# A hybrid streaming layer on one core: in the stream of attention units a tile's outputs are turned three steps behind their unit in place of two, and turns of stored and cached keys move by a step

## The chip, the core and the metric

The kernel runs on one core of a Trainium2 chip. The metric is the device time of the whole program in microseconds; lower is better. Engines are named as in the profile: PE is TensorE (matmuls, and transposes, which are matmuls with an identity), PEld its weight loads, DVE is VectorE, ACT is ScalarE, POOL is GpSimd, SP is SyncE, which only issues transfers here.

## What is computed

One inference step of one transformer layer on 1024 prompt rows and 64 new rows, with d = 1024, all in float32:

```
h = rmsnorm(x, g_mix)
qa, ka, va, qb, kb, vb, forget, gate_a, gate_b = split(h @ w_in + b_in)
A = sliding-window attention with sinks and relative bias   (8 query heads, 2 key heads, 64 wide)
B = forgetting attention, logit[t,s] += c[t] - c[s], c = cumsum(log_sigmoid(forget)), causal (8 heads)
x = x + (sigmoid(gate_a) * (A @ w_oa) + sigmoid(gate_b) * (B @ w_ob)) @ w_out
x = x + SwiGLU(rmsnorm(x));   y = rmsnorm(x, g_final)
outputs: y, and the new rows of keys, values and log forgets (kb and vb token by token)
```

The new rows also attend to 2048 cached rows of keys and values.

## The kernel before

Every large product is split: each operand is a sum of a high and a low part, and a product is three matmuls (lines L2247, L2248, L2249). The input product has 34 blocks of 128 columns in three pieces each; a piece is 24 matmuls of 320 or 384 columns. This change lies in the part of the program that the code calls the stream of units, from about 118 to 612 us of the trace.

A unit is one head of one tile of 128 queries. There are 136 units in the stream: units 0 to 71 are sliding-window ("swa"), in pairs of heads over nine tiles; units 72 to 135 are forgetting attention ("fox"), in pairs of heads over eight tiles, the later tiles with more keys. Units 2k and 2k + 1 are the two heads of one tile, and their outputs lie side by side in one slot of `o_tok`. Four units more follow the stream, for the new rows against the cache.

PE works through steps n = 0 to 135. In a step it does, in this order:

1. `turn(n)`: transposes the probabilities of unit n (L2328);
2. `scores(n + 2)`: query times keys (L2310, and L2314 for the causal mask);
3. the turns listed for this step in the table `turns_at` (below);
4. in even steps one piece of the input product ("dense", L2247 to L2249), some 3.5 to 4 us long;
5. `outputs(n - 1)`: probabilities times values (L2351) into bank 6 of `ps`.

So an odd step is short, and an even step holds a long block of matmuls that wait for nothing. The other engines follow the same steps. DVE in step n: copies half of the groups of transposed probabilities out (L562), adds the bias to scores n + 2 and takes the maximum (L1546, L1552), evacuates this step's turns (`turned_lo`), splits keys, queries or weights on some steps (L1493, L1529), and then scales the output of unit n - 1 into `o_tok` (`normalise`, L1577). ACT in step n: exp of unit n + 1 (L1086), evacuates the piece of the step before (L1073), copies the other half of the groups (L562), and makes the high parts of this step's turns (`turned_hi`).

The table has three kinds of turns, and all go through one bank, bank 7:

- `ot`, for odd n: the 128x128 slot of `o_tok` of units n - 1 and n is transposed (PE, L2363), ACT writes `ot_hi` (L1098), DVE writes `ot_lo` (L1601). POOL saves rows of them to DRAM (L893).
- `tok`, for a block of keys or values in three parts: four transposes for parts 0 and 1 (L2370), one for part 2 (L2372), then a DVE copy into `tokst` (L1589 or L1591), which POOL stores (L884, L886). ACT has no part in it.
- `cache`: four transposes of cached keys (L2377), two ACT casts (L1103), then two DVE subtractions (L1526).

Two waits of PE matter. Before any turn PE waits until the turn before it in the list has left bank 7 (`misc_done`). Before an `ot`, and before `outputs(n)`, it waits until `normalise` has written the outputs of the units ahead (`o_evac`): `ot` of unit n wants those of unit n, and `outputs(n)` wants those of unit n - 1, since all share bank 6:

```python
if k:
    pe.wait_ge(misc_done, k)
...
    pe.wait_ge(o_evac, ev[1] + 1)
...
if n >= 1:
    pe.wait_ge(o_evac, n)
```

Of the kernel before, what the change touches and what calls it, by code (L numbers as in the profile page):

```python
# [49 lines left out]
B_QA, B_KB, B_VB, B_QB, B_GATE = 2, 6, 10, 14, 18  # L50
# [57 lines left out]
N_STREAM = 136  # L108
# [81 lines left out]
def build_program(nc, x_prompt, x_sample, cache_swa_k, cache_swa_v, cache_fox_k, cache_fox_v, cache_fox_logf,  # L190
# [38 lines left out]
    with ExitStack() as ctx:  # L229
# [271 lines left out]
        turns_at = {step: [] for step in range(N_STREAM)}  # L501
        for n in range(1, N_STREAM, 2):
            if n + 2 < N_STREAM:
                turns_at[n + 2].append(("ot", n))
        for i in range(8):
            for part in range(3):
                turns_at[6 * i + 4 + 2 * part].append(("tok", B_KB + i, part))
        for c in range(4):
            turns_at[126 + 2 * c].append(("cache", 0, c))
        order = [ev for step in range(N_STREAM) for ev in turns_at[step]]  # L510
        order.append(("ot", N_STREAM - 1))
        for s in range(4):
# [2259 lines left out]
```

## Time and profile before

| | |
|---|---|
| device time, median of 3 runs | 1637.95 us (1637.29 to 1638.94) |
| the profiled execution | 1638.05 us, of which the span is 1636.3 us |
| PE busy | 1602.3 us, 98% of the span |
| DVE busy | 1018.6 us, 62% |
| ACT busy | 666.5 us, 41% |
| granted clock of PE | 0.998 of full speed over the span |

The device time is longer than the span by the 1.75 us that lie around it. Busy time of PE counts a matmul until its modelled end, and a next one starts before that; so a PE busy for 98% can still start matmuls later than it could. Starts, not busy time, are to be compared.

### The profile page before, as it was taken

The numbers are of one execution on the slowest core, as the hardware profiler recorded it, in microseconds if no ns is written. First come the engines' busy times: TensorE is split into PE (matmuls) and PEld (weight loads), VectorE is DVE, ScalarE is ACT, GpSimd is POOL, SyncE is SP. The second block draws the span as 40 slices with busy tenths as digits, with TensorE's granted clock in tenths as the row PEclk, the third lists the DMA queues.
The fourth block names the chain that finished last, engine by engine and source line by source line (L and its number), as shares of the span: only waits on it lengthen the run. The fifth ranks groups of instructions, "written<-read, shape, count | busy, mean of one in ns | idle before, by whom it ended". The sixth has DMA issues, their size and how long they took to land.

```text
span 1636.3 us, 27700 instructions
## 1 busy us (share of the span) xinstructions
PE 1602.3 (98%) x10556; PEld 1504.0 (92%) x10556; DVE 1018.6 (62%) x2232; ACT 666.5 (41%) x1333; POOL 174.7 (11%) x312
## 2 busy tenths in 40 slices
PE   7999999999999999999999999999999999999997
PEld 6999999999999999988898799999999999888886
DVE  6646555655546554436366686776677777579865
ACT  5334444544445444334253552222232222434453
POOL 3011111000000001012011000000122222110000
PEclk9999999999999999999999999999999999999999
DMA  7052331553341424659455333322344444776432
GB/s 209 26 163 100 123 109 67 185 171 92 118 138 59 123 92 149 197 185 326 151 175 177 122 91 94 118 87 73 102 156 157 157 157 150 265 229 189 144 124 89
DMA packets 190290, 230.59 MB, mean 141 GB/s; under 512 B 14807, under 2 KB 140280, under 8 KB 189640
## 3 DMA queue, kind: packets, MB, share of 16 engines
q1 hardware_dynamic: 163616, 138.71, 28.8%
q0 software_dynamic: 26544, 90.12, 15.5%
q8 instruction: 85, 1.39, 0.3%
q14 instruction: 45, 0.37, 0.1%
HBM read 166.76 MB, written 62.08 MB: 140 GB/s over the span
## 4 chain that ended last, share of the span: by engine, by line
PE 91%; DVE 4%; DMA 2%; issue 1%; ACT 1%; POOL 0%; SPq 0%; DVEq 0%; ACTq 0%; POOLq 0%
PE ps L2247 24%; PE ps L2248 24%; PE ps L2249 24%; PE ps L2351 7%; PE ps L2310 4%; PE ps L2328 3%; PE ps L2363 1%; PE ps L2532 1%; PE ps L2531 1%; DMA w_raw<-in_w_gu_dram 1%; PE ps L2269 1%; DMA w_raw<-in_w_ob_dram 1%; DVE e_lo L1897 1%; PE ps L2370 1%; PE ps L2389 0%
## 5 line engine op out<-in xcount | busy, mean ns | idle before, releaser
L2247 PE MATMUL ps<-h_hi,w_hi 128*128 128x384 f32 (+1 forms) x816 | 274.6, 337 | 1.4 <-DVE h_lo L1518 1.4
L2249 PE MATMUL ps<-h_hi,w_lo 128*128 128x384 f32 (+1 forms) x816 | 267.1, 327 | 0.0
L2248 PE MATMUL ps<-h_lo,w_hi 128*128 128x384 f32 (+1 forms) x816 | 266.9, 327 | 0.0
L2247 PE MATMUL ps<-t_hi,e_hi 128*128 128x272 f32 x704 | 202.6, 288 | 1.1 <-DVE silu L1912 1.1
L2248 PE MATMUL ps<-t_lo,e_hi 128*128 128x272 f32 x704 | 202.8, 288 | 0.0
L2249 PE MATMUL ps<-t_hi,e_lo 128*128 128x272 f32 x704 | 202.1, 287 | 0.0
L2247 PEld LDWEIGHTS ps<-h_hi,w_hi 128*128 128x128 f32 x816 | 154.1, 189 | 3.4 <-DVE h_lo L1518 1.7
L2247 PE MATMUL ps<-b_hi,e_hi 128*128 128x272 f32 x528 | 152.6, 289 | 4.5 <-ACT p L1367 1.7
L1577 DVE TENSOR_SCALAR o_tok<-ps,rinv 128x64 f32<-128x64 f32 x136 | 38.6, 284 | 189.1 <-PE ps L2351 186.9
L2248 PEld LDWEIGHTS ps<-h_lo,w_hi 128*128 128x128 f32 x816 | 154.1, 189 | 0.5 <-issue 0.5
L2249 PEld LDWEIGHTS ps<-h_hi,w_lo 128*128 128x128 f32 x816 | 153.7, 188 | 0.0
L2248 PE MATMUL ps<-b_lo,e_hi 128*128 128x272 f32 x528 | 152.1, 288 | 0.0
L2249 PE MATMUL ps<-b_hi,e_lo 128*128 128x272 f32 x528 | 151.7, 287 | 0.0
L2247 PEld LDWEIGHTS ps<-t_hi,e_hi 128*128 128x128 f32 x704 | 132.7, 188 | 1.3 <-DVE e_lo L1897 1.3
L2249 PEld LDWEIGHTS ps<-t_hi,e_lo 128*128 128x128 f32 x704 | 132.5, 188 | 0.0
L2248 PEld LDWEIGHTS ps<-t_lo,e_hi 128*128 128x128 f32 x704 | 132.4, 188 | 0.0
L1073 ACT ACTIVATE stg<-ps,bin_cols 128x384 f32<-128x384 f32 (+1 forms) x96 | 54.0, 562 | 186.9 <-PE ps L2249 186.8
L1086 ACT ACTIVATE sprob<-sprob,negm 128x256 f32<-128x256 f32 (+8 forms) x140 | 92.3, 659 | 73.5 <-DVE negm L1552 73.0
L2249 PE MATMUL ps<-e_hi,f_lo 128*128 128x512 f32 x308 | 119.8, 389 | 0.0
L2248 PE MATMUL ps<-e_lo,f_hi 128*128 128x512 f32 x308 | 119.8, 389 | 0.0
L2247 PE MATMUL ps<-e_hi,f_hi 128*128 128x512 f32 x308 | 119.8, 389 | 0.0
L1493 DVE TENSOR_TENSOR w_lo<-w_raw,w_hi 128x1024 fp32r<-128x1024 f32 x66 | 80.6, 1221 | 53.8 <-ACT w_hi L1041 53.7
(338 smaller groups left out, 3605.1 us busy)
## 6 DMA issues: line engine op xcount, KB each, us to landing
w_raw<-in_w_gu_dram SPq DMA_DIRECT2D x104, 256.0 KB, 3.3
w_raw<-in_w_in_dram SPq DMA_DIRECT2D x68, 256.0 KB, 3.2
zg_d<-stg POOLq DMA_DIRECT2D x28, 544.0 KB, 3.0
act_d<-act POOLq DMA_DIRECT2D x44, 272.0 KB, 2.8
s_d<-s_sum POOLq DMA_DIRECT2D x44, 256.0 KB, 3.4
f_raw<-s_d SPq DMA_DIRECT2D x44, 256.0 KB, 2.8
f_raw<-act_d SPq DMA_DIRECT2D x33, 256.0 KB, 2.9
w_raw<-in_w_out_dram SPq DMA_DIRECT2D x32, 256.0 KB, 3.6
```

The costliest lines, as they stand in the source:

```text
L1073: nc.scalar.activation(out, ps[:, bank_of(p), 0:c1 - c0], ACT.Identity, bias=bin_cols[:, col:col + 1]) \
L1086: nc.scalar.activation(probs, probs, ACT.Exp, bias=negm[0:R, c], accum_out=rowsum[0:R, c]).then_inc(p_ready, 1)
L1493: nc.vector.tensor_tensor(w_lo[:, slot, :], w_raw[:, slot, :], w_hi[:, slot, :].bitcast(F32), ALU.subtract) \
L1577: ins = nc.vector.tensor_scalar(o_tok[0:R, tl, HD * e:HD * e + HD], ps[0:R, 6, 0:HD], rinv[0:R, c], None, ALU.mult)
L1897: nc.vector.tensor_tensor(e_lo[:, q % RING, :], src, e_hi[:, q % RING, :].bitcast(F32), ALU.subtract) \
L2247: nc.tensor.matmul(out, l_hi, r_hi, start=start, stop=False)
L2248: nc.tensor.matmul(out, l_hi, r_lo, start=False, stop=False)
L2249: return nc.tensor.matmul(out, l_lo, r_hi, start=False, stop=stop)
L2269: last = nc.tensor.transpose(ps[:, norm_bank(tag, t, q), P * k:P * k + R], src[:, P * (4 * q + k):P * (4 * q + k) + P], ident[0:R, 0:R])
L2310: last = nc.tensor.matmul(ps[0:R, 2 + pc % 2, 0:w], lhsT, rhs, start=k == 0, stop=k == last_k and "diagonal" not in piece)
L2328: last = nc.tensor.transpose(ps[0:K, 4 + g % 2, (blk - b0) * R:(blk - b0) * R + R], score_room(u)[:, P * blk:P * blk + K], ident[0:R, 0:R])
L2351: last = nc.tensor.matmul(ps[0:R, 6, 0:w], probT[0:K, p0:p0 + R], val, start=blk == 0, stop=blk == nb - 1)
```

## The change

Three entries of the table `turns_at` are written to a later step. Nothing is added or removed.

```diff
--- before.py
+++ after.py
@@ -501,12 +501,12 @@
         turns_at = {step: [] for step in range(N_STREAM)}
         for n in range(1, N_STREAM, 2):
             if n + 2 < N_STREAM:
-                turns_at[n + 2].append(("ot", n))
+                turns_at[min(n + 3, N_STREAM - 1)].append(("ot", n))
         for i in range(8):
             for part in range(3):
-                turns_at[6 * i + 4 + 2 * part].append(("tok", B_KB + i, part))
+                turns_at[6 * i + 5 + 2 * part].append(("tok", B_KB + i, part))
         for c in range(4):
-            turns_at[126 + 2 * c].append(("cache", 0, c))
+            turns_at[127 + 2 * c].append(("cache", 0, c))
```

Before, `ot` stood in the odd steps and `tok` and `cache` in the even ones. Now `ot` stands in the even steps, ahead of the dense piece, and `tok` (steps 5 to 51) and `cache` (127 to 133) in the odd ones. The `ot` of unit 133 and that of unit 135 stay where they were.

On PE, one short odd step and the head of the even step behind it, in the first pair of heads, with `tok` part 0 or 1. Before:

```order
L2310 MATMUL ps<-ka_stack,q_lo_96 128x256
L2363 MATMUL ps<-ident,o_tok 128x128
L2351 MATMUL ps<-va_tok,probT 128x64 x2
L2328 MATMUL ps<-ident,sprob 128x128 x2
L2310 MATMUL ps<-ka_stack,q_hi_94 128x256
L2310 MATMUL ps<-ka_stack,q_lo_96 128x256
L2370 MATMUL ps<-ident,stg 128x128 x4
L2247 MATMUL ps<-h_hi,w_hi 128x384
```

The same place of the program after the change:

```order
L2310 MATMUL ps<-ka_stack,q_lo_96 128x256
L2370 MATMUL ps<-ident,stg 128x128 x4
L2351 MATMUL ps<-va_tok,probT 128x64 x2
L2328 MATMUL ps<-ident,sprob 128x128 x2
L2310 MATMUL ps<-ka_stack,q_hi_94 128x256
L2310 MATMUL ps<-ka_stack,q_lo_96 128x256
L2363 MATMUL ps<-ident,o_tok 128x128
L2247 MATMUL ps<-h_hi,w_hi 128x384
```

The transpose of `o_tok` and the four of `stg` have changed places around one `outputs`, one `turn` and one `scores`.

On DVE, the same two steps. Before:

```order
L562 COPY probT<-ps 128x256
L1546 ISA sprob,maxpart<-ps,bias,sink_rows 128x256
L1546 ISA maxpart 128x1
L1552 TENSOR_REDUCE negm<-maxpart 128x1
L1601 TENSOR_TENSOR ot_lo<-ps,ot_hi 128x128
L1568 TENSOR_TENSOR rowsum<-rowsum,sinkexp 128x1
L1569 RECIPROCAL rinv<-rowsum 128x1
L1577 TENSOR_SCALAR o_tok<-ps,rinv 128x64
L1546 ISA sprob,maxpart<-ps,bias,sink_rows 128x256
L1546 ISA maxpart 128x1
L1552 TENSOR_REDUCE negm<-maxpart 128x1
L1589 COPY tokst<-ps 128x512
```

After:

```order
L562 COPY probT<-ps 128x256
L1546 ISA sprob,maxpart<-ps,bias,sink_rows 128x256
L1546 ISA maxpart 128x1
L1552 TENSOR_REDUCE negm<-maxpart 128x1
L1589 COPY tokst<-ps 128x512
L1568 TENSOR_TENSOR rowsum<-rowsum,sinkexp 128x1
L1569 RECIPROCAL rinv<-rowsum 128x1
L1577 TENSOR_SCALAR o_tok<-ps,rinv 128x64
L1546 ISA sprob,maxpart<-ps,bias,sink_rows 128x256
L1546 ISA maxpart 128x1
L1552 TENSOR_REDUCE negm<-maxpart 128x1
L1601 TENSOR_TENSOR ot_lo<-ps,ot_hi 128x128
```

The copy of `tokst` now stands where `ot_lo` stood, behind the scores of the odd step.

On PE, a `cache` turn near the end of the stream, before:

```order
L2314 MATMUL ps<-causal_r,ident_r 128x128
L2363 MATMUL ps<-ident,o_tok 128x128
L2351 MATMUL ps<-vb_tok_115,probT 128x64 x4
L2328 MATMUL ps<-ident,sprob 128x128 x5
L2310 MATMUL ps<-k_stack_113,q_hi_95 128x512
L2310 MATMUL ps<-k_stack_113,q_lo_97 128x512
L2310 MATMUL ps<-k_stack_113,q_hi_95 128x256
L2310 MATMUL ps<-k_stack_113,q_lo_97 128x256
L2314 MATMUL ps<-causal_r,ident_r 128x128
L2377 MATMUL ps<-ident,kc_raw 128x128 x4
L2247 MATMUL ps<-h_hi,w_hi 128x384
```

After the change:

```order
L2314 MATMUL ps<-causal_r,ident_r 128x128
L2377 MATMUL ps<-ident,kc_raw 128x128 x4
L2351 MATMUL ps<-vb_tok_115,probT 128x64 x4
L2328 MATMUL ps<-ident,sprob 128x128 x5
L2310 MATMUL ps<-k_stack_113,q_hi_95 128x512
L2310 MATMUL ps<-k_stack_113,q_lo_97 128x512
L2310 MATMUL ps<-k_stack_113,q_hi_95 128x256
L2310 MATMUL ps<-k_stack_113,q_lo_97 128x256
L2314 MATMUL ps<-causal_r,ident_r 128x128
L2363 MATMUL ps<-ident,o_tok 128x128
L2247 MATMUL ps<-h_hi,w_hi 128x384
```

Here the four transposes of `kc_raw` and the one of `o_tok` have changed places.

## Rows read from the trace of the kernel before

**Rows 1.** The page, busy times: us, share of the span, instructions.

```profile
PE 1602.3 (98%) x10556; PEld 1504.0 (92%) x10556; DVE 1018.6 (62%) x2232; ACT 666.5 (41%) x1333; POOL 174.7 (11%) x312
```

**Rows 2.** Waits of the weight loads: us in total, times, longest.

```profile
PEld ps L2363 <- issue: 8.5, 33, 0.3
```

**Rows 3.** Timeline of PE, two steps: start, us, instruction, count.

```profile
201.10 0.55 PE L2351 MATMUL ps<-va_tok,probT 128*128 128x64 f32 x4
...
201.83 0.28 PE L2310 MATMUL ps<-ka_stack,q_lo 128*128 128x256 f32 x1
202.19 0.30 PE L2363 MATMUL ps<-ident,o_tok 128*128 128x128 f32 x1
202.33 0.62 PE L2351 MATMUL ps<-va_tok,probT 128*128 128x64 f32 x4
...
203.13 0.28 PE L2310 MATMUL ps<-ka_stack,q_lo 128*128 128x256 f32 x1
203.25 0.66 PE L2370 MATMUL ps<-ident,stg 128*128 128x128 f32 x4
203.66 0.39 PE L2247 MATMUL ps<-h_hi,w_hi 128*128 128x320 f32 x1
```

**Rows 4.** Timeline of DVE in the same two steps.

```profile
201.76 0.28 DVE L1577 TENSOR_SCALAR o_tok<-ps,rinv 128x64 f32<-128x64 f32 x1 [3.41 <-PE ps L2351]
...
202.84 0.15 DVE L1552 TENSOR_REDUCE negm<-maxpart 128x1 f32<-128x1 f32 x1
202.91 0.28 DVE L1601 TENSOR_TENSOR ot_lo<-ps,ot_hi 128x128 fp32r<-128x128 f32 x1
```

**Rows 5.** Lines L1589 and L1591, all: ns min/median/max, first and last start.

```profile
L1589 DVE COPY tokst<-ps x16: 681/692/692, 126.2 to 270.4; 128x512 f32<-128x512 f32 x16
L1591 DVE COPY tokst<-ps x8: 272/283/283, 139.2 to 276.1; 64x128 f32<-64x128 f32 x8
```

**Rows 6.** Timeline of PE, two steps behind a split of weights.

```profile
207.26 0.22 PE L2351 MATMUL ps<-va_tok,probT 128*128 128x64 f32 x1
...
209.88 0.42 PE L2247 MATMUL ps<-h_hi,w_hi 128*128 128x384 f32 x1
```

**Rows 7.** Timeline of PE, two steps with `tok` part 2.

```profile
194.61 0.55 PE L2351 MATMUL ps<-va_tok,probT 128*128 128x64 f32 x4
...
196.82 0.43 PE L2247 MATMUL ps<-h_hi,w_hi 128*128 128x384 f32 x1
```

**Rows 8.** Timeline, steps 127 and 128: PE, ACT and DVE around the cached keys.

```profile
569.12 0.30 PE L2363 MATMUL ps<-ident,o_tok 128*128 128x128 f32 x1
...
571.40 0.62 PE L2377 MATMUL ps<-ident,kc_raw 128*128 128x128 f32 x4
571.77 0.42 PE L2247 MATMUL ps<-h_hi,w_hi 128*128 128x384 f32 x1
...
572.05 0.58 ACT L1103 CAST ks<-ps 64x512 fp32r<-64x512 f32 x1 [0.29 <-PE ps L2377]
...
573.26 0.69 DVE L1526 TENSOR_TENSOR ks<-ps,ks 64x512 fp32r<-64x512 f32 x1 [0.58 <-ACT ks L1103]
```

**Rows 9.** Timeline of PE, steps 129 to 134, the same places.

```profile
578.20 0.29 PE L2363 MATMUL ps<-ident,o_tok 128*128 128x128 f32 x1
...
581.28 0.39 PE L2247 MATMUL ps<-h_hi,w_hi 128*128 128x320 f32 x1
...
587.49 0.28 PE L2363 MATMUL ps<-ident,o_tok 128*128 128x128 f32 x1
...
591.00 0.42 PE L2247 MATMUL ps<-h_hi,w_hi 128*128 128x384 f32 x1
...
598.31 0.28 PE L2363 MATMUL ps<-ident,o_tok 128*128 128x128 f32 x1
...
600.73 0.42 PE L2247 MATMUL ps<-h_hi,w_hi 128*128 128x384 f32 x1
```

## The prediction

> **What bounds the kernel now.** I read the busy times first: PE is busy for 1602.3 of 1636.3 us, so only what delays a start on PE can cost or give time [rows 1]. Then the waits of the weight loads, since in the stream a late matmul shows best there: the transpose of `o_tok`, L2363, waits 33 times, 8.5 us in all, at most 0.3 us each [rows 2]. Then the timeline of PE over one short odd step and the head of the even step behind it, counted from T, the start of the `outputs` that closes the step before. T is 201.10 [rows 3]. The last scores matmul starts at 201.83. The same matmul one step later, at 203.13, is followed after 0.12 us, so L2363 could start at 201.95; it starts at 202.19, T + 1.09, which is 0.24 late. The reason stands on DVE: `normalise` of that same `outputs` ends at 201.76 + 0.28 = 202.04, and 0.15 later PE goes on [rows 3, 4]. Behind it, `outputs` starts at 202.33, the place behind the next scores is reached at 203.25 (0.92 later), and the four `tok` transposes take until 203.66, where the dense piece begins, at T + 2.56.
>
> From the start of the dense piece on nothing depends on these steps until the next `outputs`. So what the change is worth in a pair of steps is how much the start of the dense piece moves against T. With 66 moved `ot` turns there are 24 such pairs with a `tok`, 11 of window attention without one, 27 of forgetting attention, and 4 with a `cache` turn.
>
> **Part 1, the wait for `normalise`.** `ot` now asks for outputs that were scaled a dense piece ago, so its own wait goes. But `outputs(n - 1)`, which now comes right behind the scores or the `tok`, shares bank 6 with the `outputs` at T and waits for the same `normalise`. Where no `tok` stands between, the wait has only moved: `outputs` starts at T + 1.09 in place of L2363.
>
> *Without a `tok`* (11 pairs of window attention, and 3 at the start of a pair of heads in forgetting attention, where scores are as short): before, the dense piece stands where the `tok` stands now, at 203.25, T + 2.15 [rows 3]. After: 1.09, then 0.92 to the place behind the scores, then one transpose. Its price lies between 0.06 (what is not hidden of 128 columns when all goes well, half of the 0.12) and 0.14 (L2363 to L2351); I take a quarter of the four, 0.41 / 4 = 0.10 [rows 3]. That is T + 2.11, a gain of 0.04, in 14 pairs 0.6 us (0 to 1.1).
>
> *The other 24 pairs of forgetting attention*: scores last long enough, L2363 did not wait, and the transpose costs the same in either place: 0, within 0.04 each, 1.0 us either way.
>
> **Part 2, the wait for bank 7.** The new thing is the distance of a `tok` in the odd step to the `ot` in the even one: no dense piece lies between any more. DVE is in order; the copy of `tokst` stands behind the scores of the odd step, where `ot_lo` stood. These follow `normalise` at T + 0.66, so their times are fixed against T: the maximum starts at 202.84 and the next instruction at 202.91, T + 1.81 [rows 4]. The transposes of `tok` are long done then (four from T + 0.85). The copy takes 0.69 for parts 0 and 1 [rows 5], ending at T + 2.50. From the end of `ot_lo` (203.19) to L2370 it was 0.06 [rows 3, 4]; from `normalise` to L2363 it was 0.15. I take 0.06, the same semaphore, and keep 0.15 as the other end. `ot` starts at T + 2.56, and the dense piece at T + 2.66.
>
> - 8 of these 16 pairs began it at T + 2.56 [rows 3]: 0.10 later each.
> - The 8 behind a split of weights at 209.88 - 207.26 = T + 2.62 [rows 6]: 0.04 later each.
>
> Sum: 0.8 + 0.3 = 1.1 us (0.5 with a transpose of 0.06; 3.2 with 0.15 and 0.14). Without the wait for the copy they would have gained 0.24 to 0.30 each; the copy eats that and some more.
>
> *The 8 pairs with part 2*: the copy takes 0.28 [rows 5], so `ot` starts at 1.81 + 0.28 + 0.06 = T + 2.15 and the dense piece at T + 2.25. Before it was 196.82 - 194.61 = T + 2.21 [rows 7]. Cost 0.04 each, 0.3 us (0 to 1.4).
>
> By the Trainium skill, page "VectorE: DVE Perf Modes", section "The TRN2 errata — SBUF-src ops pay a fixed extra latency per instruction", a VectorE instruction from PSUM takes 120 cycles and one for each element at 0.96 GHz; worked out from that page as an estimate, 512 elements take 0.66 us. The row has 0.69. By the page the 16 copies would end 0.03 earlier each and part 2 would cost 0.6 us in place of 1.1.
>
> **Part 3, the cached keys.** Here bank 7 is held longest. The casts start 572.05 - 571.40 = 0.65 behind the first transpose, the subtractions 1.21 behind the casts, two of 0.69 each follow [rows 8]. With 0.06 and the `ot` itself, 0.10, the dense piece can't start before 3.40 us behind the first `cache` transpose, which now stands where L2363 stood. In place of the dense piece's old starts:
>
> - steps 127 and 128: 569.12 + 3.40 = 572.52 against 571.77 [rows 8]: 0.75 later;
> - 129 and 130: 581.60 against 581.28 [rows 9]: 0.32;
> - 131 and 132: 590.89 against 591.00: nothing, the units are long enough by now;
> - 133 and 134: 601.71 against 600.73. These steps have one `cache` turn more than before, 571.77 - 571.40 = 0.37, which step 126 no longer has; so 601.10, and 0.61 of waiting.
>
> Sum 1.7 us (1.5 to 2.1).
>
> Behind the delayed subtractions DVE has `normalise` and the scores of the even step; these are wanted after the dense piece, 3.5 to 4 us later. ACT's exps of steps 127 to 133 start up to 1 us later and are wanted there too. If one of these covers were gone the lateness would go to PE in full. The weight splits stand 0.4 us later on DVE, for blocks wanted three pieces later. On POOL the stores of `tok` go past the save of the block, and those of `ot` come a step later; their rows are read again many steps on. SP issues the same transfers in the same order; the load of the second set of cached keys waits for the last `cache` transpose, one step later than before, and is wanted only after two units more and their dense pieces. All these I cost at nothing.
>
> **The sum.** 1.1 + 0.3 - 0.6 + 0 + 1.7 = 2.5 us more. On the profiled execution's 1638.05 that is 1640.55; the median of the runs shown is 0.10 lower, so 1640.4. All lower ends give 0.1 less than before, all upper ones 7.7 more.
>
> **The rivals.**
>
> *A, the waits vanish.* If the copy of `tokst` did not hold `ot`, the 16 pairs would start the dense piece at about T + 2.32, that is 0.24 (8) and 0.30 (8) earlier, the 8 with part 2 at 1.09 + 0.92 + 0.10 = T + 2.11, 0.10 earlier, and with 0.6 from part 1 that is 5.7 us, 1632.2. For it speaks that 8.5 us of waits stand at L2363 [rows 2]; against it that the copy stands behind the scores in the order of DVE, and 1.81 + 0.69 is more than 2.2. It needs the copy done 0.4 us earlier. Chance 0.06.
>
> *B, slower beyond doubt.* The release from DVE to PE takes 0.15, as behind `normalise`, not 0.06. That adds 0.09 to each of 24 pairs and 3 of 4 `cache` pairs: 2.4 us more, 1642.8. It decides from 0.03 us on, since 2.5 + 27 x 0.03 is 3.3. The same follows if the copy starts that much later than T + 1.81. For it: the 0.15 behind `normalise` [rows 3, 4]; against it: that was another instruction on DVE and another on PE. Chance 0.29.
>
> *C, nothing moves.* Waits change their places only and the terms of parts 2 and 3 are hidden: 1637 to 1639. It asks that the `cache` turns cost nothing, against their long hold of bank 7 [rows 8]. Chance 0.12.
>
> **How the numbers follow.** The forecast, a sum of 1 to 3.3 us, has 0.53; it and C lie within 0.2% (3.3 us, about what a measurement tells from no change): 0.65. Slower by more: B, 0.29. Faster by more: A, 0.06. The range leaves out A and the far end of B: 1637.0 to 1643.5.
>
> **What would show it.** In the changed kernel L2363 waits in the pairs with a `tok`, now for the copy of `tokst` (L1589), and behind `cache` turns for L1526, 0.3 to 0.8 us each. `outputs` (L2351) waits in the 14 pairs without a `tok`, at T + 1.09. The stretch from the first `tok` to the last is 1 to 2 us longer, steps 127 to 134 longer by 1.7 us, what lies after 620 us is the same. The prediction is wrong if `ot` starts before T + 2.4 behind a 512-wide copy, or if DVE's or ACT's lateness reaches `turn` or `outputs` behind a dense piece.

## The result, and the profile after

| | before | after |
|---|---|---|
| device time, median | 1636.95 us (1635.29 to 1638.94, 20 runs) | 1640.18 us (1638.62 to 1640.82, 20 runs) |
| ratio, with its 95% interval | | 1.0018 [1.0012, 1.0024] |
| the profiled execution | 1638.05 us, span 1636.3 us | 1639.93 us, span 1638.2 us |

By the medians the change costs 3.2 us (2.0 to 3.9 us by the interval). The forecast was 2.5 us more.

The busy times on the page of the changed kernel, as in [rows 1]:

```profile
PE 1600.2 (98%) x10556; PEld 1501.5 (92%) x10556; DVE 1016.7 (62%) x2232; ACT 666.0 (41%) x1333; POOL 175.3 (11%) x312
```

PE is 2.1 us less busy in a span that is 1.9 us longer, so the loss is waiting. Next the waits of the weight loads in the changed kernel (us in total, times, longest), to be read against [rows 2]:

```profile
PEld ps L2363 <- DVE tokst L1589: 7.3, 14, 0.8
PEld ps L2351 <- issue: 6.4, 26, 0.6
...
PEld ps L2363 <- DVE ks L1526: 1.5, 3, 0.7
...
PEld ps L2351 <- DVE probT L562: 1.1, 3, 0.4
PEld ps L2363 <- DVE tokst L1591: 0.9, 5, 0.2
```

The 33 waits of L2363 put down to "issue" are gone. In their place L2363 waits for the copy of `tokst` and for the subtractions of cached keys, and `outputs` (L2351) has waits that it took over; before it had five, 1.6 us in all. Three more, 1.1 us, are put down to DVE's copy of the probabilities (L562); they stand where a pair of heads of forgetting attention begins (415, 482 and 549 us).

The timeline of PE in the changed kernel over the odd step and the head of the even step that answer to [rows 6]. T is 206.36, the start of the `outputs` that closes the step before:

```profile
206.36 0.55 PE L2351 MATMUL ps<-va_tok,probT 128*128 128x64 f32 x4
...
207.10 0.28 PE L2310 MATMUL ps<-ka_stack,q_lo 128*128 128x256 f32 x1
207.22 0.60 PE L2370 MATMUL ps<-ident,stg 128*128 128x128 f32 x4
207.66 0.56 PE L2351 MATMUL ps<-va_tok,probT 128*128 128x64 f32 x4
...
208.40 0.28 PE L2310 MATMUL ps<-ka_stack,q_lo 128*128 128x256 f32 x1
208.93 0.33 PE L2363 MATMUL ps<-ident,o_tok 128*128 128x128 f32 x1 [0.26 <-DVE tokst L1589]
209.03 0.41 PE L2247 MATMUL ps<-h_hi,w_hi 128*128 128x384 f32 x1
```

And the timeline of DVE in the same two steps:

```profile
207.03 0.28 DVE L1577 TENSOR_SCALAR o_tok<-ps,rinv 128x64 f32<-128x64 f32 x1 [1.57 <-PE ps L2351]
...
208.11 0.15 DVE L1552 TENSOR_REDUCE negm<-maxpart 128x1 f32<-128x1 f32 x1
208.19 0.69 DVE L1589 COPY tokst<-ps 128x512 f32<-128x512 f32 x1
```

The `tok` transposes fill what was the wait for `normalise`, and nothing on PE waits in the first step. The transposes have all started by 207.66, but their copy starts only at 208.19, T + 1.83, behind the scores, and ends at 208.88. `ot` could have started at 208.40 + 0.12 = 208.52; it starts at 208.93, 0.05 behind the copy, and the dense piece at T + 2.67.

A pair without a `tok`, the timeline of PE in the changed kernel, T = 304.02:

```profile
304.02 0.55 PE L2351 MATMUL ps<-va_tok,probT 128*128 128x64 f32 x4
...
305.11 0.63 PE L2351 MATMUL ps<-va_tok,probT 128*128 128x64 f32 x4
...
305.92 0.28 PE L2310 MATMUL ps<-ka_stack,q_lo 128*128 128x256 f32 x1
306.04 0.27 PE L2363 MATMUL ps<-ident,o_tok 128*128 128x128 f32 x1
306.07 0.42 PE L2247 MATMUL ps<-h_hi,w_hi 128*128 128x384 f32 x1
306.33 0.33 PE L2248 MATMUL ps<-h_lo,w_hi 128*128 128x384 f32 x1
```

`outputs` now waits until T + 1.09, as L2363 did in [rows 3]; the dense piece starts at T + 2.05. The head of the same piece in the kernel before (T = 303.47):

```profile
303.47 0.55 PE L2351 MATMUL ps<-va_tok,probT 128*128 128x64 f32 x4
...
305.50 0.28 PE L2310 MATMUL ps<-ka_stack,q_lo 128*128 128x256 f32 x1
305.62 0.34 PE L2247 MATMUL ps<-h_hi,w_hi 128*128 128x384 f32 x1
305.79 0.34 PE L2248 MATMUL ps<-h_lo,w_hi 128*128 128x384 f32 x1
```

It starts 0.10 later, at T + 2.15. But its second matmul follows 0.17 behind the first, and in the changed kernel, behind the transpose, 0.26. So the piece of 24 matmuls lasts 4.17 us before and 4.27 after, and what the start won is given back inside the piece.

The cached keys, timeline of the changed kernel, PE and DVE, the places that answer to [rows 8, 9]:

```profile
568.91 0.62 PE L2377 MATMUL ps<-ident,kc_raw 128*128 128x128 f32 x4
...
570.78 1.39 DVE L1526 TENSOR_TENSOR ks<-ps,ks 64x512 fp32r<-64x512 f32 x2 [0.64 <-ACT ks L1103]
...
572.22 0.33 PE L2363 MATMUL ps<-ident,o_tok 128*128 128x128 f32 x1 [0.54 <-DVE ks L1526]
...
572.31 0.42 PE L2247 MATMUL ps<-h_hi,w_hi 128*128 128x384 f32 x1
...
582.12 0.39 PE L2247 MATMUL ps<-h_hi,w_hi 128*128 128x320 f32 x1
...
591.84 0.42 PE L2247 MATMUL ps<-h_hi,w_hi 128*128 128x384 f32 x1
...
602.42 0.33 PE L2363 MATMUL ps<-ident,o_tok 128*128 128x128 f32 x1 [0.30 <-DVE ks L1526]
602.51 0.42 PE L2247 MATMUL ps<-h_hi,w_hi 128*128 128x384 f32 x1
```

From the first `cache` transpose to the dense piece it is 3.40 us in steps 127 and 128, 572.31 - 568.91.

**Where the time went.** The dense pieces are the same in both kernels, so the shift of their starts, after less before, tells where time goes. It starts with an offset that is no part of the change: the first piece of the stream, with nothing moved ahead of it, starts at 119.06 before and at 117.98 after, -1.08.

| stretch | shift at its end | change in it | forecast |
|---|---|---|---|
| first piece of the stream | -1.08 | | |
| the `tok` pairs, to 282 us | +0.39 | +1.47 | +1.4 |
| pairs without `tok`, to 556 us | +0.13 | -0.26 | -0.6 |
| `cache` leaves step 126 | -0.22 | -0.35 | -0.37 |
| steps 127 to 134 | +1.78 | +2.00 | +2.05 |
| from there to 728 us | +1.81 | +0.03 | 0 |

The pieces of [rows 8, 9] start +0.54, +0.84, +0.84 and +1.78 later. Leaving step 126's gain out, the four pairs of steps cost 0.76, 0.30, 0.00 and 0.94; with it the cached keys cost 1.65. The sum over the stream is 2.86 us. The spans differ by 1.9 only, because of the -1.08 at the start.

Kernels of the experiments that leave a stretch alone give the scatter of this measure from one trace to the next. Over the pairs without `tok` three of them move against the kernel before by -0.07 (the copy made twice in the kernel before), -0.09 (only the end of the stream) and -0.38 (the copy on ACT in the kernel before). Over the `tok` pairs the two that leave them alone both move by -0.02. So the -0.26 of the pairs without `tok` is within the scatter, and the +1.47 of the `tok` pairs and the +2.00 of steps 127 to 134 are far outside it.

### The profile page after: what moved, and what is told of

Read it like the earlier page. It is cut to its first block, busy times and chain, and to the rows that moved or that the text cites. A ratio compares the mean times of both kernels' runs of the same rounds, so it can differ in the third digit from the quotient of the medians.

```text
span 1638.2 us, 27700 instructions
## 1 busy us (share of the span) xinstructions
PE 1600.2 (98%) x10556; PEld 1501.5 (92%) x10556; DVE 1016.7 (62%) x2232; ACT 666.0 (41%) x1333; POOL 175.3 (11%) x312
## 4 chain that ended last, share of the span: by engine, by line
PE 90%; DVE 6%; issue 2%; ACT 1%; DMA 1%; SPq 0%; DVEq 0%; ACTq 0%
PE ps L2247 24%; PE ps L2248 24%; PE ps L2249 24%; PE ps L2351 6%; PE ps L2310 3%; PE ps L2328 3%; PE ps L2532 1%; PE ps L2531 1%; PE ps L2363 1%; DMA w_raw<-in_w_gu_dram 1%; DVE sprob L1546 1%; DVE tokst L1589 1%; DVE e_lo L1897 1%; PE ps L2269 1%; PE ps L2389 0%
```

## The experiments

The theory on trial is H, for hold: a `tok` or `cache` turn holds bank 7 until DVE has evacuated it, and the next `ot` stands behind that. Its rivals are R1, that the loss comes from the longer odd step of DVE, which makes outputs late, and R2, that all of it lies with the cached keys. Before, measured beside these kernels, was 1637.06, 1636.86 and 1637.06 us in the three groups of runs; a ratio is always to the kernel before of its group.

### Where in the stream: the cached keys left as before

Only units up to 121 have their `ot` moved, and the cached keys keep their steps. The edit, against the changed kernel:

```diff
-                turns_at[min(n + 3, N_STREAM - 1)].append(("ot", n))
+                turns_at[n + 3 if n <= 121 else n + 2].append(("ot", n))
...
-            turns_at[127 + 2 * c].append(("cache", 0, c))
+            turns_at[126 + 2 * c].append(("cache", 0, c))
```

> The change without its last part: the turns of cached keys stay in the even steps 126 to 132, and the turns of outputs from unit 123 on stay two steps behind. Theory H (the turn of outputs is held until bank 7 is evacuated; 1.4 us in the steps with stored keys, 1.65 us in those with cached keys, 0.3 us given back elsewhere): 1.1 us slower than the kernel before, so about half of the changed kernel's loss is gone; no wait of L2363 for L1526 is left, and the waits for L1589 stay. Rival R2 (the whole loss lies with the cached keys): the same time as before. Rival R1 (the loss comes from a longer odd step on DVE, which makes outputs late): the loss shrinks by less than 1 us, and L2363 is not the line that waits.

Measured: 1638.70 us (1637.80 to 1641.41, 11 runs), ratio 1.0011 [1.0002, 1.0020]. In the trace the shift goes from -0.44 at the first piece to +0.65 behind the stream, 1.1 us more, and none of it in steps 126 to 134. L2363 has no wait for L1526; its wait for the copy is that of the full change, in the waits of this kernel's weight loads, 7.3 us in 14 times.

### The complement: only the end of the stream

Against the kernel before:

```diff
-                turns_at[n + 2].append(("ot", n))
+                turns_at[n + 2 if n < 123 else min(n + 3, N_STREAM - 1)].append(("ot", n))
...
-            turns_at[126 + 2 * c].append(("cache", 0, c))
+            turns_at[127 + 2 * c].append(("cache", 0, c))
```

> Only the last part of the change: turns of cached keys in the odd steps 127 to 133, turns of outputs from unit 123 on three steps behind, all else as before. H: 1.65 us slower than before, with the dense pieces of steps 128, 130, 132 and 134 later by 0.75, 0.3, 0 and 0.6 us. R2: 3.2 us slower, all of the loss.

Measured: 1639.25 us (1638.63 to 1640.47, 11 runs), ratio 1.0016 [1.0007, 1.0025]. The waits of this kernel's weight loads:

```profile
PEld ps L2363 <- issue: 8.4, 33, 0.3
...
PEld ps L2363 <- DVE ks L1526: 1.5, 3, 0.7
```

The pieces of steps 126, 128, 130, 132 and 134 move by -0.39, +0.76, +0.30, -0.01 and +0.94, 1.6 us in all. Both parts lose on their own, so R2 falls. By the traces they add up, 1.1 + 1.6 against 2.9 of the whole; by the medians 1.6 + 2.2 against 3.2.

### Only the steps without `tok` or `cache`

Against the kernel before:

```diff
-                turns_at[n + 2].append(("ot", n))
+                turns_at[n + 3 if 51 <= n <= 121 else n + 2].append(("ot", n))
```

> The kernel before with only those turns of outputs moved that neither a tok nor a cache turn stands near: units 51 to 121 three steps behind, all else as before. H: the wait for normalise moves from L2363 to outputs (L2351) and does not vanish; 0.3 us is given back over these steps, which the trace can show and the times can't: 0 to 1 us less than the kernel before. If the wait had vanished in these steps, 14 pairs would give 3 us and more.

Measured: 1637.26 us (1635.60 to 1638.82, 11 runs), ratio 1.0000 [0.9991, 1.0009]. The times can't tell 0.3 us. In the trace the dense pieces are shifted by -0.30 up to the last piece before the moved turns and by -0.51 behind them; this 0.21 is no more than the scatter given above, so that a gain is not shown. The waits show that the wait moved and did not go:

```profile
PEld ps L2363 <- issue: 5.6, 22, 0.3
...
PEld ps L2351 <- issue: 3.9, 14, 0.6
...
PEld ps L2351 <- DVE probT L562: 1.1, 3, 0.4
```

Before it was 8.5 us at L2363 [rows 2] and 1.6 us at L2351. 2.9 us of waits went from the one, and 3.4 came at the other.

### What holds bank 7: the copy of `tokst` on ACT

In the changed kernel the same 24 copies are made by ACT, ahead of its exp, and DVE has none (the lines for part 2 are left out here):

```diff
+                    if part < 2:
+                        ins = nc.scalar.copy(tokst[:, 4 * part:4 * part + 4, :], ps[:, 7, :].rearrange("p (t c) -> p t c", t=4))
...
-                    if part < 2:
-                        ins = nc.vector.tensor_copy(tokst[:, 4 * part:4 * part + 4, :], ps[:, 7, :].rearrange("p (t c) -> p t c", t=4))
```

> The changed kernel with the copy of tokst (24 of them) on ACT in place of DVE. H: the copy can start at about T + 1.5 (behind the transposes), ends by T + 2.1, and the turn of outputs no longer waits for it: the dense pieces of the 16 pairs with parts 0 and 1 start at about T + 2.25 in place of T + 2.65, those of the 8 with part 2 about 0.15 earlier, some 7 to 8 us less than the changed kernel, about 1632.5, faster than the kernel before by 4 us. If the two waits of PE were not what costs, the time stays within 1 us of 1640.

Measured: 1631.94 us (1631.58 to 1634.04, 9 runs), ratio 0.9973 [0.9963, 0.9983]. The timeline of PE and ACT in this kernel, T = 203.88; the lines of PE stand one number lower here, so that L2362 is the transpose of `o_tok` and L2246 the dense piece:

```profile
203.88 0.55 PE L2350 MATMUL ps<-va_tok,probT 128*128 128x64 f32 x4
...
204.74 0.60 PE L2369 MATMUL ps<-ident,stg 128*128 128x128 f32 x4
...
205.44 0.59 ACT L1096 COPY tokst<-ps 128x512 f32<-128x512 f32 x1
...
205.91 0.28 PE L2309 MATMUL ps<-ka_stack,q_lo 128*128 128x256 f32 x1
206.08 0.33 PE L2362 MATMUL ps<-ident,o_tok 128*128 128x128 f32 x1
206.18 0.41 PE L2246 MATMUL ps<-h_hi,w_hi 128*128 128x384 f32 x1
```

ACT starts 0.70 behind the first transpose instead of 0.97, and the dense piece at T + 2.30. In most of the pairs where ACT has no weights to split it starts at T + 2.22, and behind part 2 between T + 1.83 and T + 2.24. Added up over the 24 pairs, the pieces start 7.4 us sooner past T than in the changed kernel; the medians give 8.2.

The Trainium skill, page "VectorE: DVE Perf Modes", section "The TRN2 errata — SBUF-src ops pay a fixed extra latency per instruction", gives ScalarE 172 cycles and one for each element at 1.2 GHz for a source in PSUM; as an estimate, 512 elements take 0.57 us. The row has 0.59, so the trace agrees.

### The same engine, the other order: the copy ahead of the scores

DVE keeps the copy, but makes it first in its step, ahead of the bias and the maximum:

```diff
+                early = [ev for ev in turns_at[n] if ev[0] == "tok"]
+                for ev in early:
+                    turned_lo(ev)
...
-                    turned_lo(ev)
+                    if ev not in early:
+                        turned_lo(ev)
```

> The changed kernel with the copy of tokst on DVE one place earlier in its step, ahead of the scores of the odd step; DVE has the same work. H: the copy starts at about T + 1.5 in place of T + 1.81, so the 16 dense pieces start 0.3 us earlier and the 8 with part 2 up to 0.2: some 5 to 6.5 us less than the changed kernel, about 1634, and 3 us less than the kernel before. R1 (it is the load of DVE in the odd step that costs): no gain, or slower, since scores come 0.7 us later.

Measured: 1633.54 us (1631.74 to 1634.27, 9 runs), ratio 0.9977 [0.9967, 0.9987]. The timeline of PE and DVE in this kernel, T = 204.03, the lines of PE four numbers higher (L2367 turns `o_tok`, L2251 is the dense piece):

```profile
204.03 0.55 PE L2355 MATMUL ps<-va_tok,probT 128*128 128x64 f32 x4
...
205.52 0.69 DVE L1589 COPY tokst<-ps 128x512 f32<-128x512 f32 x1 [0.19 <-PE ps L2374]
...
206.13 0.48 DVE L1546 CUSTOM_DVE_ANT_0 sprob<-ps,bias,sink_rows 128x256 f32<-128x256 f32 x1
...
206.27 0.33 PE L2367 MATMUL ps<-ident,o_tok 128*128 128x128 f32 x1
206.37 0.41 PE L2251 MATMUL ps<-h_hi,w_hi 128*128 128x384 f32 x1
```

DVE does the same work as in the changed kernel, and its pass over the scores of the step comes 0.9 us later (206.13, T + 2.10, against T + 1.23), yet the kernel is 6.6 us faster than that one. So it isn't the length of DVE's odd step that costs but the time of the one copy: R1 falls.

### Is the order needed at all: the copy on ACT in the kernel before

The edit of "What holds bank 7", made in the kernel before.

> The kernel before, with nothing but the copy of tokst on ACT in place of DVE: the control for the gain seen with it. H: in the kernel before a dense piece lies behind each tok turn, so its evacuation holds nothing; within 0.5 us of the kernel before. R1 (less work on DVE is what helped): faster by several us here too.

Measured: 1636.73 us (1636.11 to 1637.72, 11 runs), ratio 0.9999 [0.9991, 1.0008]. In the waits of its weight loads the transpose of `o_tok` (L2362 here) waits as before:

```profile
PEld ps L2362 <- issue: 8.4, 33, 0.3
```

The faster copy alone is worth nothing. With a dense piece between the `tok` turn and the next `ot`, nobody waits for it.

### The size of the hold: the copy made twice

One edit in both kernels: the copy of parts 0 and 1 is made twice, so that DVE and bank 7 are held for 0.69 us more, 16 times.

```diff
+                        chained(nc.vector.tensor_copy(tokst[:, 4 * part:4 * part + 4, :], ps[:, 7, :].rearrange("p (t c) -> p t c", t=4)))
```

In the changed kernel:

> The changed kernel, with the copy of tokst for parts 0 and 1 (16 of them) made twice on DVE, one behind the other. H: the second copy, 0.65 to 0.75 us, stands on the path in full: 16 times, 10 to 12 us more than the changed kernel, about 1651.

Measured: 1651.61 us (1650.74 to 1652.27, 4 runs), ratio 1.0089 [1.0075, 1.0103]. That is 11.4 us over the changed kernel, or 0.71 for each of 16 copies. In the waits of its weight loads (L2364 turns `o_tok`):

```profile
PEld ps L2364 <- DVE tokst L1590: 19.1, 16, 1.7
```

In the kernel before:

> The same doubled copy in the kernel before. H: a dense piece of 3.5 us and more lies between the tok turn and the next turn; the second copy is hidden there, and nothing changes (within 0.5 us of the kernel before). R1: DVE falls behind in either kernel, and some 10 us are lost here too.

Measured: 1637.27 us (1636.02 to 1639.47, 10 runs), ratio 1.0002 [0.9993, 1.0011]. The same 11 us of DVE work cost nothing there.

### What the experiments point to

The `ot` turns moved up to unit 121, the cached keys as before, the copy of `tokst` on ACT:

> Both cures together: the copy of tokst on ACT, and the turns of cached keys (with the outputs from unit 123 on) left where the kernel before has them. H says that the two terms are independent and add: 1.65 us less than the changed kernel with the copy on ACT, so about 1630.3, 6.7 us less than the kernel before. If they are not independent, it stays at 1632.

Measured: 1630.56 us (1630.02 to 1630.73, 5 runs), ratio 0.9960 [0.9947, 0.9974]. It is 6.3 us faster than the kernel before and the fastest of all kernels here: it keeps the moved `ot` turns and leaves out what held them. Against the changed kernel with the copy on ACT it is 1.4 us less by the medians; in the traces the dense piece of step 134, counted from the first piece of the stream, is shifted by -6.2 where that one has -4.6. So the two terms add.

## Why the prediction held

The path was forecast rightly, and so was the sign. The nearness of the sum is in part luck: two errors in the `tok` stretch cancel, as shown below.

**The wait for `normalise` (part 1).** As forecast it went from L2363. At T + 1.09 it came back at `outputs` in most of the pairs of window attention without a `tok`, and in six of the eight pairs with part 2 as well. In the three pairs at the start of a pair of heads, which the prediction counted with them, `outputs` waits for something else and longer: for the copy of the probabilities (L562), 0.36 us each.

The gain of 0.6 us was mis-sized: the trace shows 0.26, and 0.21 in the kernel that moves only these turns, both within the scatter between traces, so that it is not shown that anything was won. The step that failed is "from the start of the dense piece on nothing depends on these steps", and with it the price of the transpose, 0.10. The second matmul of a piece starts 0.26 us behind the first where a transpose stands ahead of it and 0.17 where scores do (384 columns both), so a pair like that at 306 wins 0.10 at the start of the piece and loses 0.09 behind its first matmul. From the last scores matmul to the second matmul of the piece it is 305.79 - 305.50 = 0.29 before and 306.33 - 305.92 = 0.41 after: counted so, the transpose costs 0.12, about the 0.14 that it cost in its old place, and nearly nothing is won. In the pairs with a `tok` a transpose stood ahead of the piece before the change too, and there the starts are a fair measure.

What is left of the 0.26 comes from three pairs of window attention whose pieces start 0.17 to 0.24 sooner past T (at 287.80, 312.39 and 330.64), and part of it goes in two pairs behind the tile of the 64 new rows (294.29 and 349.88). The prediction counted none of these apart. In the last two `ot` is 64x64, and the piece starts 0.20 behind it, at T + 2.12 and T + 2.40 where it was T + 2.02 and T + 2.24. Of the 0.24 at 312.39 and 330.64, 0.14 is a delay that the unchanged steps don't always have: in the kernel before with the copy on ACT, the same in these steps, both pieces start that much sooner.

**The wait for bank 7 (part 2).** The mechanism held, and so did the times of a usual pair. In 12 of the 16 pairs with a full copy it starts at T + 1.81 to T + 1.83 (forecast 1.81), `ot` 0.05 behind its end (0.06), and the dense piece at T + 2.63 to T + 2.68 (2.66). Behind part 2 the piece starts at T + 2.23 to T + 2.25 in six of eight (2.25). The turns are shifted by one step, so that three pairs have to be compared as a sum. For the pairs of [rows 3, 6, 7] it is 2.21 + 2.56 + 2.62 = 7.39 us past T before and 2.65 + 2.25 + 2.67 = 7.57 after, 0.18 more, and eight times that is 1.4.

That the stretch as a whole came to +1.47 is luck all the same, since the prediction took these three pairs for all. Added up over all 24, the pairs with a `tok` start their pieces 60.9 us past T after the change and 58.9 before: 2.0 us more, and not 1.4. Four pairs carry more than this surplus, with pieces at T + 2.81 (176.75 and 236.12), T + 2.90 (216.19) and T + 2.99 (255.93). In the first two `ot` is 64x64 and the piece stands 0.20 behind it. In the other two the copy itself starts late, for 255.93 because the outputs of its unit were scaled late on DVE:

```profile
252.94 0.55 PE L2351 MATMUL ps<-va_tok,probT 128*128 128x64 f32 x4
...
253.97 0.28 DVE L1577 TENSOR_SCALAR o_tok<-ps,rinv 128x64 f32<-128x64 f32 x1 [1.46 <-PE ps L2351]
...
255.10 0.69 DVE L1589 COPY tokst<-ps 128x512 f32<-128x512 f32 x1
```

All four are late in the kernel with the cached keys left as before too. But in the changed kernel with the copy made twice the last two start at T + 3.38 like their neighbours, so their lateness is not part of the hold; its cause stays open. Against the surplus stands the first pair of the stretch, which has lost its `tok` and got none. Before:

```profile
123.23 0.33 PE L2351 MATMUL ps<-va_tok,probT 128*128 128x64 f32 x2
...
125.57 0.40 PE L2247 MATMUL ps<-h_hi,w_hi 128*128 128x320 f32 x1
```

After:

```profile
122.15 0.33 PE L2351 MATMUL ps<-va_tok,probT 128*128 128x64 f32 x2
...
123.99 0.39 PE L2247 MATMUL ps<-h_hi,w_hi 128*128 128x320 f32 x1
```

It goes from T + 2.34 to T + 1.84 and wins 0.50 us, where the prediction gave such a pair 0.04.

The copy on ACT and the copy ahead of the scores show that it is this copy's time that costs, and the doubled copy that every further 0.69 us of it reaches the end in full. By the page "VectorE: DVE Perf Modes" of the Trainium skill, section "The TRN2 errata — SBUF-src ops pay a fixed extra latency per instruction", which the prediction cites, the copies would be 0.03 shorter; the row has 0.69, as before.

**The cached keys (part 3).** 0.76, 0.30, 0.00 and 0.94 against 0.75, 0.32, 0 and 0.98 forecast (0.61 of waiting and 0.37 for the turn that moved in), less 0.35 against 0.37 for step 126. The sum is 1.65 against 1.7. It carries over half of the loss.

**The rivals.** A (the waits vanish, 1632.2) did not happen. The kernel with the copy out of the way takes 1631.94, but that is no proof of A's price: A's sum leaves the 1.7 us of the cached keys out, which that kernel still pays, and has the 0.6 of part 1 in it. With both put right it would be 3.4 us under the kernel before, where 5.1 were measured; the gain at the first pair (0.50) and the earlier pieces behind part 2 (down to T + 1.83, where A has T + 2.11) are not in it.

B named two things that would push it past 3.3 us. The slower release of 0.15 is refuted: it was 0.05 behind each of the 16 full copies. That the prediction took 0.06 was luck in part, since it was read where PE had not waited: L2370 at 203.25 is just 0.12 behind the scores matmul at 203.13, as without any wait. The copy's start was 0.02 late at most in the usual pair and T + 1.82 in the mean of all 24, short of the 0.03 that B asked for. C fell with the 1.65 us of the cached keys.

**The sum.** 2.5 us forecast, 2.86 in the traces, 3.2 by the medians. What was missed is the 0.3 of part 1; in the `tok` stretch 0.6 too little and 0.5 too much stand against each other. The other 0.4 between traces and medians is within the interval of 2.0 to 3.9 us.

## What to carry to other kernels

A wait that stands in front of a turn may be moved into other work, but ask what now stands between two users of the same bank. Here the long dense piece between a wide turn and the next one hid the whole evacuation, and the change put both into the short step. Where users have to be close together, the evacuation must be first in its engine's step, or on an engine that is free; each 0.1 us that it comes later is 0.1 us of PE.

Count from a fixed start (T) and compare starts, not waits. The waits of L2363 grew by little in total, from 8.5 to 9.7 us, and said nothing of the sign; the starts did. Add them up over all pairs, the first and the last of a stretch too, and not over one pair taken as the pattern. A start is a fair measure only where the same kind of instruction stands ahead of it, as part 1 shows; otherwise count to the second matmul or to the end of the block behind it.

## What the runs showed of the hardware that I had not expected

- The release to PE takes 0.05 us behind a copy from PSUM on DVE (208.88 to 208.93), on ACT (206.03 to 206.08) and behind the subtraction (572.17 to 572.22). Behind `normalise` it is 0.15 in both kernels (202.04 to 202.19 before, 304.96 to 305.11 after). I didn't find out why.
- A transpose costs PE in a place where its own row doesn't show it. The dense piece starts 0.03 us behind a transpose that had not waited (306.04 to 306.07), but its second matmul comes 0.26 behind its first, instead of 0.17. Behind a transpose that had waited the piece starts after 0.08 to 0.10, and the second matmul again after 0.26 (with 320 columns it is 0.23 behind a transpose and 0.15 behind scores).
- The time ahead of the stream, where the kernels are the same, differs between executions: the first dense piece starts at 119.06, 117.98, and 118.78 in three of them (before, after, and only the steps without `tok`). One trace of each kernel can't be compared by its span when 1 us matters.
